# Experts' weights with neighbouring rows in one partition

## What is computed

```python
p_group = softmax(hf @ w_group + b_group)              # 4 groups, the best one is taken
fine = (hf @ w_router + b_router).reshape(N, 4, 8)     # 8 experts in a group, the best two
...
def expert_block(args):
    xblk, e = args
    gt, up = jnp.split(xblk @ w_gu[e], 2, axis=-1)     # w_gu[e]: 1024 x 512
    return (jax.nn.silu(gt) * up) @ w_down[e]          # w_down[e]: 256 x 1024
...
out = zeros.at[tok_buf].add(yb * w_buf[:, None])       # weighted sum over a token's two experts
```

## Time and profile before

| | |
|---|---|
| median of 3 runs | 2256.4 us (2255.75 to 2259.95) |
| the profiled execution | 2261.5 us, span 2259.7 us |
| PE busy | 2032.8 us (90%) |
| DVE busy | 1044.4 us (46%) |
| ACT busy | 620.6 us (27%) |
| POOL busy | 101.0 us (4%) |
| moved by DMA | 266.85 MB, 147157 packets |
| gate-up loads of the experts | 32 of 2048 KB |
| down loads of the experts | 32 of 1024 KB |

### The profile page before, as it was taken

The page is one execution under the profiler, slowest core; times in us unless marked ns, Lnnn a source line. Parts: engine busy times, 40 slices in busy tenths (PEclk is TensorE's granted clock), DMA queues, the critical chain, the costliest instruction groups (busy, mean ns, idle before and its releaser), DMA issues. The chain is left out here.

```text
span 2259.7 us, 29226 instructions
## 1 busy us (share of the span) xinstructions
PE 2032.8 (90%) x12216; PEld 1427.8 (63%) x12216; DVE 1044.4 (46%) x1913; ACT 620.6 (27%) x1180; POOL 101.0 (4%) x119
## 2 busy tenths in 40 slices
PE   8989999999999899999999898877999999677773
PEld 4466688888854674888888676666666677322331
DVE  2276554446345764554463565564254344411113
ACT  1165222223221662222232333332153121000001
POOL 0000000000000000000000000111000000011102
PEclk9999999999999999999999999999999999688996
DMA  8100245323222100332222311000111234699994
GB/s 277 55 21 1 75 163 209 138 86 111 66 103 87 35 1 1 118 106 93 94 104 74 112 66 50 3 3 23 38 56 38 79 108 171 248 372 394 385 381 180
DMA packets 147157, 266.85 MB, mean 118 GB/s; under 512 B 8871, under 2 KB 71694, under 8 KB 146702
## 3 DMA queue, kind: packets, MB, share of 16 engines
q1 hardware_dynamic: 140686, 250.24, 31.4%
q0 software_dynamic: 5760, 12.59, 1.6%
q10 hardware_dynamic: 576, 2.10, 0.2%
HBM read 258.61 MB, written 27.26 MB: 127 GB/s over the span
## 5 line engine op out<-in xcount | busy, mean ns | idle before, releaser
L237 PE MATMUL ps<-arena 64*64 64x64 f32 (+11 forms) x6448 | 880.5, 356 | 125.1 <-DMA arena<-in_moe_w_gu 47.6
L237 PEld LDWEIGHTS ps<-arena 64*64 64x64 f32 (+3 forms) x6448 | 467.3, 153 | 500.8 <-issue 376.3
L247 PE MATMUL ps<-arena 128*128 128x128 f32 (+3 forms) x1182 | 163.6, 284 | 47.3 <-DVE arena L859 17.2
L395 DVE TENSOR_SCALAR arena<-arena 128x1024 int32<-128x1024 int32 (+1 forms) x204 | 138.1, 677 | 144.4 <-PE ps L243 83.3
L247 PEld LDWEIGHTS ps<-arena 128*128 128x128 f32 (+3 forms) x1182 | 134.9, 145 | 96.0 <-issue 48.8
L241 PE MATMUL ps<-HTr,WH0r 128*128 128x512 f32 (+1 forms) x448 | 169.8, 379 | 1.2 <-ACT T16r L1046 1.2
L241 PE MATMUL ps<-HTr,WH1r 128*128 128x512 f32 (+1 forms) x448 | 169.8, 379 | 1.2 <-ACT T16r L1046 1.2
L402 ACT ACTIVATE WH0r<-arena 128x1024 fp32r<-128x1024 f32 x86 | 91.5, 1063 | 214.1 <-DVE slot2r L398 92.3
L243 PE MATMUL ps<-T16r,WH0r 128*128 128x512 f32 (+1 forms) x384 | 144.1, 375 | 0.0
L243 PE MATMUL ps<-T16r,WH1r 128*128 128x512 f32 (+1 forms) x384 | 144.1, 375 | 0.0
L402 ACT ACTIVATE WH1r<-arena 128x1024 fp32r<-128x1024 f32 x82 | 87.2, 1064 | 197.1 <-DVE slot0r L398 106.1
(11 more groups left out here) (371 smaller groups left out, 2813.9 us busy)
## 6 DMA issues: line engine op xcount, KB each, us to landing
arena<-in_moe_w_gu SPq DMA_DIRECT2D x32, 2048.0 KB, 17.2
arena<-in_w_gate_up SPq DMA_DIRECT2D x44, 1024.0 KB, 7.0
arena<-in_moe_w_down SPq DMA_DIRECT2D x32, 1024.0 KB, 15.7
arena<-in_w_down SPq DMA_DIRECT2D x8, 2048.0 KB, 7.8
arena<-in_w_in SPq DMA_DIRECT2D x7, 2048.0 KB, 8.5
arena<-in_w_in SPq DMA_DIRECT2D x9, 1024.0 KB, 5.5
arena<-in_w_o SPq DMA_DIRECT2D x4, 2048.0 KB, 7.9
arena<-in_w_down SPq DMA_DIRECT2D x4, 1536.0 KB, 6.6
```

The lines of the kernel that those rows point to most:

```text
L237: return e.matmul(o, l, r, start=start, stop=stop, skip_group_check=True)
L247: return e.transpose(o, i, ident[0:n, 0:n])
L395: e.tensor_scalar(h.bitcast(I32), raw.bitcast(I32), -4096, None, ALU.bitwise_and).then_inc(*v_half.up(*name, "mask"))
```

## The change

In `expert_weights` row p * 8 + k of the gate-up matrix now goes to partition p, place k, and row p * 2 + k of the down matrix likewise: eight, or two, neighbouring rows of DRAM lie behind one another in a partition, one stretch of 16 KB, or 8 KB. To match, the turns of `p_expert_x` take columns k, k + 8, k + 16, ... of the gathered rows in place of 128 neighbouring ones, and those of `p_expert_down` every second hidden value. The gain has to come in the same order; it gets a small tile `fg` of its own and a load of its own in `sync`, between the router's weights and the positions. The number of loads, their bytes, the products and the waits stay.

```diff
@@ -207,7 +207,7 @@
 
         sink, qkg, rb = small(12), small(128), small(36)
         rw = small(288).rearrange("p (k n) -> p k n", n=36)
-        posi, nhalf, nsink = small(4), small(8), small(12)
+        posi, nhalf, nsink, fg = small(4), small(8), small(12), small(8)
         eps6 = 1e-6
 
 
@@ -2399,17 +2399,17 @@
         ACTB, THm = [[at(f"{n}{q}", c + 256 * q, 256) for q in range(2)] for n, c in (("ACTB", 12928), ("THm", 13952))]
         AT_ = [at(f"AT{q}", 13440 + 256 * q, 256).rearrange("p (k t) -> p k t", k=2) for q in range(2)]
         Wgu, Wdn = I["moe_w_gu_2"][0], I["moe_w_down_2"][0]
-        fg = gcol("ffn_norm_g_2")
         HALF = (slice(0, 64), slice(64, 128))
         expert_of = lambda n, x: n + 16 * x
 
         def expert_weights(e, w, n, x):
 
+
             if n < 16:
-                return w[expert_of(n, x)].rearrange("(k p) n -> p k n", p=P)
+                return w[expert_of(n, x)].rearrange("(p k) n -> p k n", p=P)
             j = n - 16 + 8 * x
             r = e.value_load(ebi[0:1, j:j + 1].bitcast(I32), min_val=0, max_val=31)
-            return w[bass.ds(r, 1), :, :].rearrange("o (k p) n -> p (o k) n", p=P)
+            return w[bass.ds(r, 1), :, :].rearrange("o (p k) n -> p (o k) n", p=P)
 
         def s_gate_up(e, u):
             if u >= 5:
@@ -2458,7 +2458,7 @@
                 bk = bank(e, ("xT", n, hf), v_mo, ("xT", n, hf))
                 e.wait_ge(*d_gat[n % 3][n])
                 for k in range(4):
-                    t = tr(e, bk[:, k * P:(k + 1) * P], xg[:, (4 * hf + k) * P:(4 * hf + k + 1) * P])
+                    t = tr(e, bk[:, k * P:(k + 1) * P], xg.rearrange("p (q k) -> p k q", k=8)[:, 4 * hf + k, :])
                 t.then_inc(*p_mo.up("xT", n, hf))
 
         def v_expert_x(e, n):
@@ -2495,7 +2495,7 @@
             bk = bank(e, ("aT", n), a_mo, ("aT", n))
             e.wait_ge(*v_mo["a", n])
             for k in range(2):
-                t = tr(e, bk[:, k * P:(k + 1) * P], a[:, k * P:(k + 1) * P])
+                t = tr(e, bk[:, k * P:(k + 1) * P], a.rearrange("p (q k) -> p k q", k=2)[:, k, :])
             t.then_inc(*p_mo.up("aT", n))
             w = [WDN[(2 * n + x) % 5].rearrange("p (k n) -> p k n", k=2) for x in range(2)]
             for u in (2 * n, 2 * n + 1):
@@ -2642,6 +2642,7 @@
             e.dma_start(rw[:, :, 0:4], w3(I["moe_w_group_2"][0], 0, 8, 0, 4), allow_slow_non_contiguous=True).then_inc(
                 *d_small.up("all"))
             e.dma_start(rw[:, :, 4:36], w3(I["moe_w_router_2"][0], 0, 8, 0, 32)).then_inc(*d_small.up("all"))
+            e.dma_start(fg, I["ffn_norm_g_2"][0].rearrange("(p k) -> p k", k=8)).then_inc(*d_small.up("all"))
             e.dma_start(posi.bitcast(I32), I["positions_2"][0].rearrange("(i p) -> p i", p=P),
                         allow_slow_non_contiguous=True).then_inc(*d_small.up("all"))
 
```

## The result

| kernel | median of its runs, us | ratio to the kernel before, 95% interval |
|---|---|---|
| before | 2256.4 | |
| after | 2241.5 (2240.1 to 2244.0) | 0.9921 (0.9906 to 0.9935) |
| after, once more on another occasion | 2243.8 (2241.3 to 2247.5), beside it before 2260.6 | 0.9932 (0.9919 to 0.9946) |

The forecast was 2243.3, with a range of 2237.5 to 2251; the medians lie 14.9 us apart, and the two ratios stand for 12 to 21 us. The profiled execution took 2244.0 us, its span is 2242.2.

The account below looks back on a forecast made before the run. DMA engines were taken to bound the experts' stage. 26 gate-up loads at 0.45 us plus 25 down loads at 0.07 gave 13.5, over 1.032 13.1 us, off 2256.4: 2243.3 us, range 2237.5 to 2251.

Parts of the forecast that it names:

- The bound: Experts' stage: full DMA engines set the pace until block 15 starts; block period falls from 17.5 to 16.5 us.
- A 16 KB piece: Gate-up loads: a piece takes 620 ns, so a load takes 4.96 us in place of 5.41.
- The line through 4 and 12.6 KB: Piece prices in loads: 0.0373 ns a byte between 162 and 480 ns, extended to 8 and 16 KB.
- The gate-up term of the sum: Paced stretch: 26 gate-up loads, 6 to 31, each 0.45 us shorter in engine time.
- Two steps of the sum: Gate-up loads before cost 84.6 ns per 2 KB piece; engine time counts at 1.032 of the clock's.
- An 8 KB piece: Down loads: a piece takes 315 ns, so each of 25 loads takes 2.52 us in place of 2.59.
- The turns: Stepped operand reads on PE: 0 taken, bounded by 0 to 3.5 us for 30 turns on the path.
- Rival B: Stepped reads in the turns cost double, 3.5 us back, giving 2246.8 us; chance 0.13.
- The head: Start of the experts' stage: `hn_scr` writes take 12.5 us in place of 4.0, yet stay hidden, cost 0.
- Rival E: Each `hn_scr` piece waits for two long ones, DVE stands 7 us, giving 2250.3 us; chance 0.09.
- SP doesn't run dry: SP's load order in the stage: queued loads still cover the wait for down products, under 1 us to spare.
- Rivals C and D: Weight loads: C, pieces aren't joined, 2256.4 us, chance 0.07; D, memory serves 16 KB stretches worse, 2269.6 us, chance 0.08.

Follow-up runs that it names:

- half the bytes: Changed kernel loading only inner places 0 to 3 of 8 of each gate-up tile from load 6 on; median 2197.4 us, ratio 0.9732.
- the run of the gate-up weights alone: Kernel before with only gate-up weights in 16 KB pieces and row turns stepped by 8; median 2240.5 us, ratio 0.9942.
- the other order on SP: Changed kernel with the next block's gate-up loads issued ahead of this block's down loads; median 2228.9 us, ratio 0.9869.
- the down pieces alone: Kernel before with only down weights in 8 KB pieces and hidden-value turns stepped by 2; median 2259.3 us, ratio 1.0004.
- the run with 4 KB pieces: Gate-up weights in 4 KB pieces (two neighbouring rows), row turns stepped by 2, down weights as in the kernel before; median 2249.3 us, ratio 0.9966.
- the run with the other order and gate-up pieces only: Next block's gate-up loads issued ahead of down loads, gate-up in 16 KB pieces, down in 4 KB as before; 2231.8 us, ratio 0.9876.

## Why the prediction was right

**The bound.** The mechanism was right: DMA paced the stage and still does. 13 waits for gate-up weights, 47.6 us, became 12 and 34.0, against "about 34" in the forecast, and half the bytes removed nearly all of them. The period of a block from 1993.01 to 2191.78 in twelve blocks is 16.56 us, forecast 16.5. PE's own need was put too high, at 14.1: it held up-products of 8.62 us, which ran at a mean granted clock of 0.81 (2049.5 to 2058 us); at 1.00 they take 7.09. With half the bytes a block took 12.4.

**A 16 KB piece.** A stretch of the changed kernel with gate-up pieces alone, 2004 to 2007 us, packets and share of the 16 engines:

```profile
DMA packets 90, 1.29 MB, mean 429 GB/s; under 512 B 11, under 2 KB 11, under 8 KB 11
q1 hardware_dynamic: 83, 1.29, 100.2%
```

79 pieces (90 less 11 small): 1.002 x 3 x 16 / 79 = 609 ns, forecast 620. By the packet records, the mean of all 3,328 such pieces from gate-up load 6 to the start of block 15 is 620. The line through 4 and 12.6 KB held. The gate-up term of the sum, 26 x 0.45 / 1.032 = 11.3 us, came out as 12.9 in the run of the gate-up weights alone.

**Two steps of the sum were wrong, and they cancel.** The forecast priced the 2 KB pieces in a quiet stretch, and it turned the engines' time into the clock's with one factor, 1.032, before and after. The whole stage shows neither. The queues of SP and POOL in the changed kernel, 1980 to 2187 us:

```profile
q1 hardware_dynamic: 7166, 78.92, 92.2%
q0 software_dynamic: 3600, 6.49, 8.2%
```

A gate-up load and a down load together are 3.146 MB. They cost each engine 0.954 x 225 x 3.146 / 80.55 = 8.38 us before and 0.922 x 207 x 3.146 / 78.92 = 7.61 us after, 0.77 less; the forecast had 8.00 and 7.48, 0.52 less. The missing part is the 2 KB piece: the mean of the stretch's 26,624 is 88.5 ns, not 84.6, and 26 x 64 x 3.9 ns are 6.5 us. Against that, the shares of the two queues add up to 1.030 before and to 1.004 after, since packets overlap less. In the clock's time a pair of loads fell from 8.38 / 1.030 = 8.14 to 7.61 / 1.004 = 7.58 us, 0.56 less, and 25.5 pairs give 14 us, as measured. With the overlap unchanged they would have given 0.77 x 25.5 / 1.032 = 19. So one step left out some 6 us of gain and the other some 5 us of loss. That 13.1 lies within a microsecond or two of the 14.0 and 14.8 measured is luck; that the loads' pieces set the time is not. Why 2 KB pieces are dearer within the stage, and why long pieces overlap less, no run took apart.

**An 8 KB piece: a small term.** The forecast had 315 ns and 1.7 us for all down loads. A stretch of the changed kernel in which down pieces run alone, 2008.5 to 2011.5 us:

```profile
DMA packets 157, 1.16 MB, mean 388 GB/s; under 512 B 17, under 2 KB 17, under 8 KB 17
q1 hardware_dynamic: 157, 1.16, 102.0%
```

140 pieces: 1.020 x 3 x 16 / 140 = 350 ns. With the other order on SP, 1999.5 to 2001.5 us:

```profile
DMA packets 164, 0.85 MB, mean 426 GB/s; under 512 B 57, under 2 KB 57, under 8 KB 63
q1 hardware_dynamic: 115, 0.83, 98.5%
```

101 pieces: 0.985 x 2 x 16 / 101 = 312 ns. So the line holds for 8 KB too, but not in every place. Nor does it hold everywhere for 4 KB. Down pieces of 4 KB alone, in the run of the gate-up weights alone, 2038.5 to 2041.5 us:

```profile
DMA packets 260, 1.01 MB, mean 337 GB/s; under 512 B 13, under 2 KB 13, under 8 KB 260
q1 hardware_dynamic: 259, 1.01, 96.5%
```

247 pieces: 0.965 x 3 x 16 / 247 = 188 ns, where the forecast took 162. Over the whole stretch, from load 6 to the start of block 15, the mean of a down piece was 168.6 ns with 4 KB before and 328 ns with 8 KB after. That is 8 x (2 x 168.6 - 328) = 74 ns a load, the 0.07 us of the forecast.

In time it is harder to see. What all down loads are worth came out as 1.5 us lost with them alone, and as 1.1 and 1.9 us gained beside long gate-up pieces (231.8 against 230.7 and 229.9), with 1.7 forecast; with the other order 2.0. One execution of a kernel differs from the next by 0.5 to 0.8 us in this column, so the sign isn't certain. With the down pieces alone the engines' work for a pair of loads falls too, from 8.38 to 0.944 x 223 x 3.146 / 79.36 = 8.35 us (1980 to 2203 us), but the shares of the queues add up to 1.020 in place of 1.030, and that takes more than it gives. Why pieces of down loads stand longer in some stretches, and hardly with the other order, isn't settled: it may be what is in flight beside them, and no run took that apart.

**The turns.** Taken at 0, measured 0.009 us each, 0.3 us in all. Rival B named the right place and a wrong price: the load of stationary columns does get slower by 39%, but it lies under the product of the turn before. By the Trainium skill, "SBUF — State Buffer", section "Door 1: The DMA port swizzle", an access that gets fewer than two hits on a 16-byte line pays. A penalty is there, at a step of 8. But a step of 2 leaves two float32 on a line, and it pays at least the same, so the measurement doesn't bear out the limit of two. The last four turns of the kernel, of hidden values only:

```profile
L247 PEld LDWEIGHTS ps<-arena x4: 196/205/216, 2200.5 to 2205.2; 128*128 128x128 f32 x4
```

Before, these four took 138 to 143 ns. In the run with 4 KB pieces, where eight of ten turns have a step of 2, the median of all is 209 ns and ten turns take 1.44 us.

**The head.** The writes of `hn_scr` compete piece by piece with longer pieces, as forecast; their landing, DVE's passing of its wait, and the landing of the gathers of rows:

```profile
L2185 ACTq DMA_DIRECT2D hn_scr<-arena x4: 326/336/348, 1902.3 to 1919.7; - x4
...
DMA to landing us min/median/max: 2.6/6.7/12.8
...
L2346 DVEq EVENT_SEMAPHORE  x1: 21/21/21, 1938.0 to 1938.0; - x1
...
DMA to landing us min/median/max: 3.3/14.8/16.5
```

The slowest write lands 12.8 us after its issue, where it was 8.7. The last is issued at 1919.7, so it has landed by 1932.6, and DVE passes at 1938.0 without idle time. The forecast had the landing near 1938 and 3 us in hand; it was 5. By the packet records the 256 pieces of the last two writes ran from 1921.1 to 1931.4, 10.4 us, where they ran from 1923.9 to 1929.0 before; the forecast had 12.5 us from 1924 on. The duration was near, the start was not; why they start earlier isn't shown. Rival E didn't happen. The gathers took 14.8 us at the median in place of 7.8, hidden by the three blocks that they are ahead.

**SP doesn't run dry.** Forecast with under 1 us to spare. The rate in the stretch was 412 GB/s; what a 16 KB piece at 609 ns allows is 16 x 16384 / 609 = 430 GB/s without the down pieces. Nothing in the waits of PE shows a stall by SP's order in the steady state; most of the price of the order lay at the head, and the forecast took that for given.

**The rest of the difference.** Of the 17.5 us between the two profiled spans, 14.0 are paced, 2.5 the front, and 1.7 the tail, less 0.8 in the head. In the tail the up-products of block 15 take 8.75 us after a wait of 2.83, where they took 9.80 after 4.28; in other runs 7.09. The granted clock shows it, in the changed kernel at the start of block 6, after a wait of 3.50, and of block 7, after 1.02 (columns as in the earlier trace rows):

```profile
2043.00:2048.00 5.00, 5.00 (x14) 1.58 (x12) 0.00 (x0) 0.00 (x0) 0.11 (x1) 0.50 1.05 434
2060.00:2065.00 5.00, 5.00 (x26) 2.07 (x24) 0.00 (x0) 0.00 (x0) 1.80 (x2) 1.00 1.00 403
```

0.50 is 1.2 GHz, 1.00 is 2.4 GHz. Here the wait of 1.02 us didn't cost the clock, and that of 3.50 did. In between, the length of the wait alone doesn't tell: the up-products of block 14 took 7.09 us after a wait of 2.30 in the run with the other order and gate-up pieces only, and 8.78 us after 2.16 in the first run of the other order. The forecast left this out of the tail; it is worth 1 us here and up to 2.7.

Rivals C and D fell with the first rows: the packet count, and 609 ns against D's deciding 677.

## What to carry to other kernels

Where DMA paces a stage, price one piece of a load from stretches in which one size runs alone, fit a fixed part and a part for each byte, and count only the loads that lie between the first wait and the last. Then hold the prices against the whole stage, the queue's share times the time over its bytes: here that work was 5% above the sum of the quiet prices before the change and 2% after it, and the part of the share above 1.00 went away. From 2 to 4 KB a piece brought half of what 2 to 16 KB brought. The layout that makes rows neighbours in a partition cost some 0.3 us elsewhere, since an operand is then read with a step. Then look for idle time ahead of the paced stretch: here the order of issues was worth about as much as the pieces (13.2 against 14.0 us), and the two add up.

## What the runs showed of the hardware

- A piece alone costs about 8 ns and 0.037 ns a byte on one of the 16 engines: 84.6, 162, 480 ns for 2, 4 and 12.6 KB, 609 for 16 KB. Within the busy stage the means are 88.5 ns for 2 KB, 168.6 for 4 KB (down loads), 328 for 8 KB and 620 for 16 KB.
- The summed packet time of a full stage is 1.03 of 16 engines' time with 2 and 4 KB pieces and 1.00 with 16 and 8 KB, so such shares can't be carried over from one piece size to another.
- Pieces of one size and kind differ by place: 8 KB down pieces took 350 ns in one stretch and 312 in another, 4 KB down pieces up to 188 ns where they take 162 elsewhere.
- Turns whose stationary columns have a step of 2 or of 8 float32 load in 185 to 216 ns in place of 138 to 146, and cost the turn 0.009 us.
- Beside a queue with 16 KB pieces in place of 2 KB ones, the slowest 512 KB write took 12.8 us instead of 8.7, and a gather 14.8 instead of 7.8 at the median.
